# A 512-column matmul over the high and low part of the first 256 tokens, with the key products of the decode moved to eighths 55 to 62

## What is computed

```python
h = RMSNorm_pre(x)
p = h @ w_in                     # one projection, 2048 x 8208
q_a, k_a, v_a, z_a, qkv_b, z_b, beta_in, a_in = split(p)
# mixer A: dilated windows (128,1), (512,4), (2048,16), 8 heads x 128, rotary on 32 dims;
#          the samples attend to cached keys and values
# mixer B: gated DeltaNet, 8 heads: causal conv of width 4 + SiLU on q/k/v, delta rule in chunks
o_a, o_b = mixer_A(...) * silu(z_a), mixer_B(...) * silu(z_b)
y = x + RMSNorm_post(concat(o_a, o_b) @ w_out)
```

## Time and profile before

| | |
|---|---|
| runs | 1330.28, 1328.22, 1330.18 us; median 1330.18 |
| the profiled execution's own time | 1330.15 us |
| its span, first to last instruction | 1328.3 us |
| TensorE matmuls | 1258.6 us busy, 95%, 10094 instructions |
| VectorE | 768.2 us, 58% |
| ScalarE | 543.2 us, 41% |
| GpSimd | 288.5 us, 22% |
| DMA | 151.71 MB, 82695 packets, mean 114 GB/s |

### The profile page before, as it was taken

One profiled execution on the slowest core, in us unless ns is written; L12 is line 12 of the kernel. 1 busy time (PEld: TensorE's weight loads), 2 busy tenths in 40 slices (PEclk: granted clock), 3 DMA queues, 4 the chain that ended last, 5 costly groups with the idle time before them and its releaser, 6 DMA issues. The chain is left out here.

```text
span 1328.3 us, 28169 instructions
## 1 busy us (share of the span) xinstructions
PE 1258.6 (95%) x10094; PEld 1212.4 (91%) x10094; DVE 768.2 (58%) x1872; ACT 543.2 (41%) x1472; POOL 288.5 (22%) x271
## 2 busy tenths in 40 slices
PE   4999998999999999999999999999999998899997
PEld 4989998999899989998999899989998997889997
DVE  6466367537653765377537653765376556474445
ACT  6352344434443444344434443444344444412210
POOL 1123112321232123212321232123112311122210
PEclk9999999999999999999999999999999998899998
DMA  6331434243324342434243324332434254312353
GB/s 226 92 96 51 137 105 146 55 146 108 129 55 147 106 130 58 138 113 136 66 138 111 122 66 138 116 118 66 138 117 132 66 185 143 98 65 95 95 192 129
DMA packets 82695, 151.71 MB, mean 114 GB/s; under 512 B 8793, under 2 KB 27330, under 8 KB 81026
## 3 DMA queue, kind: packets, MB, share of 16 engines
q1 hardware_dynamic: 72222, 144.87, 34.2%
q10 hardware_dynamic: 10384, 5.50, 1.6%
HBM read 132.20 MB, written 17.27 MB: 113 GB/s over the span
## 5 line engine op out<-in xcount | busy, mean ns | idle before, releaser
L553 PE MATMUL PJ<-h_hi,w_hi 128*128 128x264 f32 (+1 forms) x2432 | 723.3, 297 | 1.2 <-ACT memx L981 1.2
L554 PE MATMUL PJ<-h_lo,w_hi 128*128 128x264 f32 (+1 forms) x2432 | 689.9, 284 | 0.0
L555 PE MATMUL PJ<-h_hi,w_lo 128*128 128x264 f32 (+1 forms) x2432 | 688.3, 283 | 0.0
L553 PEld LDWEIGHTS PJ<-h_hi,w_hi 128*128 128x128 f32 x2432 | 462.5, 190 | 17.8 <-issue 12.4
L554 PEld LDWEIGHTS PJ<-h_lo,w_hi 128*128 128x128 f32 x2432 | 462.7, 190 | 2.8 <-issue 1.7
L555 PEld LDWEIGHTS PJ<-h_hi,w_lo 128*128 128x128 f32 x2432 | 460.9, 190 | 0.0
L1858 POOL TENSOR_TENSOR w_lo<-w_raw,w_hi 128x512 fp32r<-128x512 f32 x160 | 210.1, 1314 | 887.8 <-ACT w_hi L954 887.8
L954 ACT ACTIVATE w_hi<-w_raw 128x512 fp32r<-128x512 f32 x320 | 197.7, 624 | 102.7 <-PE PJ L555 84.1
L1364 DVE TENSOR_TENSOR w_lo<-w_raw,w_hi 128x512 fp32r<-128x512 f32 x160 | 114.0, 718 | 117.5 <-ACT w_hi L954 113.9
L981 ACT ACTIVATE memx<-PJ 128x264 f32<-128x264 f32 (+2 forms) x130 | 49.2, 379 | 71.9 <-PE PJ L555 60.5
L1223 ACT ACTIVATE mem<-MX 128x256 f32<-128x256 f32 x48 | 18.4, 384 | 116.6 <-PE MX L755 116.0
(11 more groups left out here) (317 smaller groups left out, 1618.8 us busy)
## 6 DMA issues: line engine op xcount, KB each, us to landing
w_raw<-in_w_in SPq DMA_DIRECT2D x256, 256.0 KB, 2.7
w_raw<-in_w_out SPq DMA_DIRECT2D x64, 256.0 KB, 2.8
kv<-in_cache_win_k SPq DMA_DIRECT2D x24, 512.0 KB, 3.6
kv<-in_cache_win_v SPq DMA_DIRECT2D x16, 512.0 KB, 3.8
mem<-in_x_prompt SPq DMA_DIRECT2D x4, 1024.0 KB, 10.4
S<-in_state_delta SPq DMA_DIRECT2D x8, 512.0 KB, 3.5
out<-S SPq DMA_DIRECT2D x8, 512.0 KB, 3.7
out<-mem ACTq DMA_DIRECT2D x16, 256.0 KB, 3.3
```

Source lines behind the costliest of these rows:

```text
L553: pe.matmul(out, wh, h_hi[:, k, tok], start=k == 0, stop=False)
L554: pe.matmul(out, wh, h_lo[:, k, tok], start=False, stop=False)
L555: last = pe.matmul(out, wl, h_hi[:, k, tok], start=False, stop=k == KT - 1)
```

## The change

1. h_hi and h_lo become one tensor h2, and for each k of a first half one matmul of 512 columns (the 256 tokens' high and low part side by side) takes the place of L553 and L554. It fills the whole bank; w_lo with h_hi adds to its first 256 columns. It holds for all tiles of the projections but the first two and the interleaved ones at the start of the output projection. VectorE adds the two halves of the bank by a reduce at segment 4 (`half_out`) and takes over the guards; ScalarE's copy of the first half goes. TensorE waits for `proj_half` in place of `proj_sb` there.
2. New keys, values and convolution rows are written by channel straight from xk, xv and xq by SyncE; the samples' q by an access pattern that swaps its two dimensions. L650, L651, L652, L658, L702 and the ScalarE copies and DMAs behind them go. The host transposes the outputs.
3. The key products of a head stand at steps 55 to 62 of its own stretch (`decode_keys`), with their loads moved in SyncE's queue. The decode after the last head starts 14 steps earlier (`late=-14`).
4. VectorE's list has mix_b ahead of own_b. Row 9 of the gated matrix gets another buffer and is loaded early; rows 10 to 14 and the value loads are issued ahead of the weight load of the same step.

```diff
-ROW_GROUPS = ((0, 1, 2, 3, 4, 5, 6, 8), (9, 10, 11), (12, 13, 14))
+ROW_GROUPS = ((0, 1, 2, 3, 4, 5, 6, 8, 9), (10, 11), (12, 13, 14))
-        h_hi = sb("h_hi", [P, KT, TT], F32R)
-        h_lo = sb("h_lo", [P, KT, TT], F32R)
+        h2 = sb("h2", [P, 2, KT, TT], F32R)
+        h_hi, h_lo = h2[:, 0], h2[:, 1]
...
+                both = PJ[:, 0, :].rearrange("p (a t) -> p a t", a=2)
+                wide = half == 0 and not (isinstance(T, int) and T < 2)
...
+                    elif not end:
+                        pe.matmul(both, wh, h2[:, :, k, tok], start=k == 0, stop=False)
+                        last = pe.matmul(ps, wl, h_hi[:, k, tok], start=False, stop=False)
...
+            def half_out(h, j):
+
+                T = NT * h + (T_H + j)
+                dst, off = DST[j]
+                guard(h, j)
+                dve.wait_ge(s["proj_ps"], made(T, 0))
+                dve.tensor_reduce(dst[:, off:off + SPLIT], PJ[:, 0, :].rearrange("p (a t) -> p t a", a=2), AX.X,
+                                  ALU.add).then_inc(s["proj_half"], 1)
...
+                        if seg == 4 and not (isinstance(h, int) and h == 0 and j == 0):
+                            half_out(h, j)
...
+            def attn_rows(h):
+                yield from idle(47)
+                if not first:
+                    sp.wait_ge(s["pv_sum"], h)
+                keys(0)
+                yield from idle(2)
                 sp.wait_ge(s["qrow_out"], 16 * h + 16)
+                sp.dma_start(qb[:], scratch_q[h].rearrange("b d -> (b d)").partition_broadcast(P)).then_inc(s["qb_in"], 16)
...
+            def conv_out(h):
+
+                yield from idle(9)
+                for j in range(3):
+                    sp.wait_ge(s["proj_sb"], 16 * h + (2 * j + 4))
+                    sp.dma_start(c_new[h, j], xq[:, TP:3 + TT]).then_inc(s["crow_out"], 16)
+                    yield from idle(8)
+
+            def attn_out(h):
+
+                yield from idle(46)
+                sp.wait_ge(s["q_ok"], h + 1)
+                sp.dma_start(scratch_q[h].rearrange("b d -> d b"), xa[:, TP:TT],
+                             allow_slow_non_contiguous=True).then_inc(s["qrow_out"], 16)
+                yield from idle(7)
+                sp.wait_ge(s["k_ok"], h + 1)
+                sp.dma_start(k_new[h], xk).then_inc(s["k_out"], 16)
+                yield from idle(5)
+                sp.wait_ge(s["proj_sb"], 16 * h + 16)
+                sp.dma_start(v_new[h], xv).then_inc(s["v_out"], 16)
...
-                stretch(h, [tail_a(h - 1), attn_decode(h - 1, sums=(24, 4, 3)), own_b(h), own_a(h), mix_b(h), mix_q(h),
-                            delta_decode(h)])
+                stretch(h, [tail_a(h - 1), mix_b(h), own_b(h), own_a(h), mix_q(h), delta_decode(h),
+                            attn_decode(h - 1, sums=(22, 4, 3)), decode_keys(h)])
...
-            work = [later(tail_a(NH - 1)), attn_decode(NH - 1)]
+            work = [later(tail_a(NH - 1)), attn_decode(NH - 1, late=-14)]
```

More of the change, by code:

```diff
@@ L498, in _ @@
             for n in range(40):
+                step(work)
                 if n % 2 == 0 and n < 8 * PARTS:
@@ L502, in _ @@
                     load_out(slot + 2, p)
-                step(work)
             over(work)
@@ L542, in _, with segment @@
         def _(pe):
-            def segment(T, par, half, q, first=False):
+            def segment(T, par, half, q, first=False, out=False):
                 if half == 0:
@@ L559, in segment, with project @@
                     last.then_inc(s["w_used"], 1)
-            def project(T, par, work, first=False):
+            def project(T, par, work, out=False):
                 for half in range(2):
                     for q in range(NQ):
-                        segment(T, par, half, q, first)
+                        segment(T, par, half, q, out=out)
                         step(work)
@@ L690, in tail_a @@
                 last.then_inc(s["attn_ps"], 1)
-            def own_b(h):
-                for j in range(3):
-                    yield from idle((11, 7, 8)[j])
-                    pe.wait_ge(s["proj_sb"], 16 * h + (2 * j + 4))
-                    if j == 0 and (not isinstance(h, int) or h > 0):
-                        pe.wait_ge(s["vtok_ok"], 2 * h)
-                        pe.wait_ge(s["crow_ok"], 3 * h)
-                    elif j > 0:
-                        pe.wait_ge(s["crow_ok"], 3 * h + j)
-                    pe.transpose(MD[0:11, 1, 0:P], xq[:, 3 + TP - 3:3 + TT], ident[:]).then_inc(s["crow_ps"], 1)
             def mix_b(h):
@@ L845, in delta_decode, with attn_decode @@
                               stop=True).then_inc(s["d_outer"], 1)
-            def attn_decode(hh, sums=12):
-                yield from idle(17)
-                pe.wait_ge(s["vtok_ok"], 2 * hh + 2)
+            def attn_decode(hh, late=0, sums=12):
+                yield from idle(17 + late)
+                pe.wait_ge(s["vtok_ok"], hh + 1)
                 pe.wait_ge(s["qkp"], hh + 1)
@@ L976, in copy_out @@
             def copy_out(T, half, dst, off=0):
+                late = not (isinstance(T, int) and T < 2)
                 act.wait_ge(s["proj_ps"], made(T, half))
+                if late:
+                    act.wait_ge(s["proj_half"], T - 1)
                 o = off + half * SPLIT
@@ L1171, in own_b @@
             def own_b(h):
-                for j, m in enumerate((1, 2, 0)):
-                    yield from idle((11, 4, 5)[j])
-                    act.wait_ge(s["crow_ps"], 3 * h + j + 1)
-                    if j > 0 or not isinstance(h, int) or h > 0:
-                        act.wait_ge(s["crow_out"], 32 * (3 * h + j))
-                    act.activation(rows, MD[0:11, 1, 0:P], ACT.Copy).then_inc(s["crow_ok"], 1)
-                    yield
+                for j in range(3):
+                    yield from idle((12, 5, 6)[j])
                     act.wait_ge(s["conv_ok"], 3 * h + j + 1)
@@ L1723, in attn_decode @@
                     last.then_inc(s["red"], 1)
-                yield
-                yield
+                    yield
+            def attn_decode(hh, late=0, sums=(9, 1, 4)):
+                yield from idle(17 + late)
                 dve.wait_ge(s["sc_T"], hh + 1)
@@ L1799, in y_half @@
                     link(dve.tensor_tensor(sz[:, tok], PJ[:, half, 0:WIDTH[half]], y_ch[:, j, tok], ALU.add))
+                elif wide and half == 0:
+                    link(dve.tensor_reduce(sz[:, tok], PJ[:, 0, :].rearrange("p (a t) -> p t a", a=2), AX.X, ALU.add))
                 else:
```

238 lines of the change are left out of this document (105 added, 133 removed).

## The result

The changed kernel takes **1377.12 us** (median of 4 runs, 1376.50 to 1378.01), the kernel before 1330.23 in the same rounds (4 runs): ratio 1.0354, 95% interval 1.0336 to 1.0372. I had forecast 1280, in 1266 to 1301. The profiled run took 1376.50 us, its span is 1374.6.

The account below looks back on a forecast made before the run. The prediction took TensorE, busy for 95% of the span, to bound the kernel. Its terms, -25.4 - 8.8 - 5.8 + 2.8 + 3.6 - 6.5 - 9.9 = -50.0, took 1330.15 us to 1280, range 1266 to 1301.

Parts of the forecast that it names:

- Part 1: Projection tiles: merging two 256-column matmuls into one of 512 saves 21.5 ns, 1184 times, 25.4 us in all.
- My own counter-evidence: Evidence for the rivals on projection matmuls: surplus stays, 1290 us (chance 0.25), or no saving, 1303 us (0.05).
- SyncE's new DMAs: SyncE's queue: the added output DMAs of each head wait for things already due and cost 0.
- The rival of the late query: Samples' q, 1024 single elements, delays VectorE at step 55: slower, 1335 us; chance 0.05 together with late sums.
- Part 5: Wait at L727, once per head: TensorE arrives 0.45 us earlier and waits that much longer, 3.6 us given back.
- Part 3: Key products moved into their own head's steps: L854's wait goes, 5.8 us saved, at no cost to the recurrence.
- Part 4: VectorE's sums of the bank halves delay the block inverse's first step (L755) by 0.35 us a head: +2.8 us.
- Part 2: TensorE, per head: ten transposes taken out, 80 in all at 0.11 us, 8.8 us saved.
- Part 6: Behind the last head: two holes, each followed by half clock, close, saving 6.5 and 9.9 us.
- the first hole: Tail, TensorE stopped at 1101.23 because row 9 of the gated matrix came late; loading it early saves 6.5 us.
- TensorE waits for the recurrence: Sign of being wrong in kind: TensorE waiting for the recurrence in steps 55 to 62; no size given.
- The output tiles: Output projection tiles, nothing but matmuls, should shrink from 11.48 us to near 11.1; otherwise wrong in kind.

Follow-up runs that it names:

- e17: e16 with 14 of 16 merged pairs of each wide half issued as three 256-column matmuls again: 1288.35 us.
- e18: e16 run again unchanged, in the same rounds as e17: 1285.32 us.
- e1: The changed kernel with the samples' query written as 128 rows of 32 bytes instead of 1024 single elements: 1322.26 us.
- e3: The changed kernel, single elements kept, with the first key load moved from step 47 to step 51, behind the query's broadcast: 1339.38 us.
- e16: e11 with VectorE's L1561 (the scaled values) also moved ahead of the third convolution's second half: 1284.77 us.
- e12: e11 with row 9 of the gated matrix loaded late again and the last head's decode 14 steps later again: 1301.08 us.
- e11: e1 with VectorE's second half of the third convolution and ScalarE's sigmoid of that convolution each one step later: 1291.89 us.
- e8: The changed kernel with the query's single-element write issued at step 51, behind k's swap, and the broadcast and second key load behind it: 1394.78 us.
- e13: e11 with an added unread write per head of 128 single elements into 512 contiguous bytes: 1338.58 us.
- e14: e11 with an added unread write per head of 1024 single elements, each 64 bytes from the next: 1293.68 us.
- e15: e11 with the query written a second time per head, unread, in 128 rows of 32 bytes: 1292.08 us.
- e9: The changed kernel writing only the first sample's query, 128 single elements in one 512-byte row, and reading that row back eight times: 1394.96 us.

## Why the prediction was wrong, step by step

**Part 1, the merged matmul: mis-sized, 3 to 6 us in place of 25.4.** TensorE in the output tiles, 15 pairs of 512 + 256 columns from the first row to the last:

```profile
1240.38 0.40 PE L589 MATMUL PJ<-h,w_hi 128*128 128x512 f32 x1
1240.61 0.28 PE L590 MATMUL PJ<-h,w_lo 128*128 128x256 f32 x1
...
1245.63 0.28 PE L592 MATMUL PJ<-h,w_lo 128*128 128x256 f32 x1
```

5.25 us / 15 = 350.0 ns a pair, 5.2 ns less than three matmuls, where I had 21.5; x 1184 are 6.2 us, and 3.0 were measured in e17 and e18 for 1036 pairs. 512 columns take 350.0 - 118.4 = 231.6 ns, 18.3 above the bare stream (the starts themselves lie 234 and 117 ns apart, median of 1110 pairs). The step that failed is the inference from the earlier trace rows: slow passes of ordinary 32-bit data and a stretch at half clock have no surplus, so I held that a long stream hides it. The surplus grows with the columns instead, from 11.7 to 18.3 ns. My own counter-evidence, that 264 columns cost 2.3 ns more than 256, was right and deserved more than 0.30. By the rule that I cited from the Trainium skill (TensorE: Matmul & The Clock Gate, Back-to-back issue gap) the merge would save 3 us. That it comes near is no support for it: its level is off at both sizes (109.2 ns against 118.4, 215.8 against 231.6), and the section gives it for a matmul by itself and says that at few columns it counts too little, since it leaves out the weight loads.

**SyncE's new DMAs, "0": the step that cost the forecast.** The term was 0; with rows of 32 bytes in its place (e1) the kernel is 54.9 us faster. I looked at when they are issued and who waits for them, and priced the one for q at 33 ns a piece. The rival of the late query had the cause and the sign, but the wrong place (step 55 instead of the swap at step 49), and a price by the piece, for which I gave it 0.05. The row behind the 33 ns is a mean over a queue whose pieces have 530 bytes on average (5.50 MB / 10384); it says nothing about elements that lie side by side. The elements' own packets take 9 ns each by the trace, less than I had; what they cost shows behind them. The DMA of e3, from 278.5 to 287.5 us, which is behind the elements' write (issued at 276.64), in 40 slices:

```profile
DMA  3000000000320410000000000122820240003302
```

and of the changed kernel from 281.5 to 290:

```profile
DMA  3162602206000502017034900940508006902099
GB/s 21 19 96 77 58 19 39 39 0 58 19 19 0 39 19 39 19 19 58 39 39 19 96 19 0 58 19 19 39 19 39 0 0 58 39 19 19 19 77 58
```

Each digit is the busy share of the 16 engines in tenths. In e3 most slices are empty while a weight load (8.4 us to landing), the swap and the query's write are all under way. In the changed kernel the engines count as 41% busy in this stretch, but the keys trickle at a mean of 34 GB/s: its 70 packets over 512 bytes take 0.79 us each on average. In e1 the like stretch, from 274 to 277.5 us, moves 168 GB/s, with 0.18 us for such a packet. So a busy share does not show this stall, whether it is low or high; the time to landing does.

**Part 5, L727's wait: right in kind, 7.7 us in place of 3.6, and the clock left out.** I held that VectorE's chain keeps its 9.0 us, since the work is the same set in another order. It takes 9.8, from L1514 at 359.50 to L745 at 369.32. VectorE there:

```profile
365.96 0.23 DVE L1521 TENSOR_SCALAR memx<-cw 128x8 f32<-128x8 f32 x1
366.23 1.44 DVE L1524 SCALAR_TENSOR_TENSOR memx<-cw,memx 128x8 f32<-128x8 f32 x2
367.71 0.23 DVE L1524 SCALAR_TENSOR_TENSOR memx<-memx,cw 128x8 f32<-128x8 f32 x1
```

and GpSimd:

```profile
366.39 1.26 POOL L1855 TENSOR_TENSOR w_lo<-w_raw,w_hi 128x512 fp32r<-128x512 f32 x1 [6.80 <-ACT w_hi L972]
```

The second of the two small operations takes 1.18 us instead of 0.23 and ends when GpSimd's operation ends (367.65). The Trainium skill (GPSIMD Engine Reference, Specifications) says that GpSimd shares its SBUF interfaces with VectorE, and that instructions with two SBUF inputs contend; the trace agrees, 1.18 us against 0.23 for an operation with two such inputs. It is so in 7 of the 8 heads. The kernel before has the same meeting in 7 heads (1.27 us, from 337.30 in the head of the earlier trace rows), but in the second convolution, before its chain starts at 343.04; the new order moved it into the chain. The longer wait also costs more clock. Before:

```profile
350.00:355.00 5.00, 3.00 (x17) 3.01 (x18) 3.06 (x7) 3.75 (x10) 1.28 (x1) 0.79 0.08 33
355.00:360.00 5.00, 5.00 (x38) 5.00 (x38) 1.38 (x2) 1.65 (x4) 1.27 (x1) 0.87 0.43 138
```

and e1, where nothing else is in the way (the number behind the engines is the granted clock):

```profile
352.00:357.00 5.00, 2.93 (x14) 2.93 (x15) 3.71 (x9) 2.25 (x4) 0.39 (x1) 0.59 0.16 56
357.00:362.00 5.00, 5.00 (x33) 5.00 (x33) 1.39 (x2) 1.19 (x3) 1.27 (x1) 0.72 0.37 105
```

In 10 us of each, (0.21 + 0.13) x 5 x 2 = 3.4 us at half clock before and (0.41 + 0.28) x 5 x 2 = 6.9 in e1: 1.7 us more are lost in this head, about 14 in eight if the others are like it. The whole trace bears this out: over the seven heads between the landmarks the granted clock is 0.991 before and 0.974 in e1, 8.5 and 23.9 us lost, 15 more. I had priced half clock at the tail only.

**Part 3, the key products: right.** L854's wait of 5.8 us went, as said, and the cover that I cost at 0 held: in e1 no wait of the recurrence itself is left.

**Part 4, the sums: right.** 2.8 forecast, 2.3 measured (L773).

**Part 2, the transposes: 4.5 us given back that I had not counted.** 80 of them are gone from the trace; their 8.8 us were not tested alone. But L820 waits 5.7 us in all, where L802 waited 1.2. Before, the end of the recurrence on TensorE:

```profile
290.42 0.39 PE L795 MATMUL MX<-small,mem 128*128 128x128 f32 x2
...
292.29 0.60 PE L657 MATMUL MD<-ident,memx 128*128 128x128 f32 x4
292.72 0.27 PE L658 MATMUL MD<-ident,memx 128*8 128x128 f32 x1
293.15 0.66 PE L802 MATMUL MX<-ident,mem 128*128 128x128 f32 x4 [0.15 <-DVE mem L1628]
```

and now:

```profile
307.92 0.39 PE L813 MATMUL MX<-small,mem 128*128 128x128 f32 x2
...
310.65 0.66 PE L820 MATMUL MX<-ident,mem 128*128 128x128 f32 x4 [0.71 <-DVE mem L1623]
312.59 0.60 PE L687 MATMUL MD<-ident,memx 128*128 128x128 f32 x4
```

Both take 2.73 us from the recurrence's last result to L802 or L820, so VectorE is no slower; it even idles 0.81 us ahead of L1611, so the key products do not delay it. What changed is TensorE's work in between: L658 is gone, and the four transposes of the values, which stay for attention, stand one step later (L687). So these five transposes at 0.11 us ran where TensorE would otherwise have waited: taking them from there saves nothing, and the four that moved cost their time anew. The wait stays in e16 (6.0), so it is not the elements' doing.

**Part 6, the tail: the sum came near, its cause only in part.** 16.4 forecast; 15.6 between the landmarks of the two traces, and this holds part 1 in the output tiles too. e12 undoes both edits and gives back 9.2, not 16.4. From the last landmark to the end pass 240.3 us before, 236.2 in e12 and 226.9 in e11: some 9 us are these two edits, some 4 others. The wait of the last decode is back in e12 (6.2 us), which bears out the decode's part. The wait of the first hole is 1.95 us in e12 as in e11, 2.95 before. So row 9's group is not what shortened it, and my 6.5 for it is not borne out; which other edit did it was not tried.

**The sum again**, for the kernel without the bad write (e1, 42 us above my 1280): part 1 some 19 to 22, the wait at L745 4, the clock behind it some 14, L820 4.5. These make 42 to 45. The tail, about 4 short of my figure beside what part 1 lost there, would make it 46 to 49, so the pieces are estimates and some 4 to 7 us of them are counted twice or made good elsewhere. The bad write adds 55.

Of my signs, "TensorE waits for the recurrence" came true, but at step 53, just ahead of the steps that I named (in e8 at the key products). The output tiles shrank from 11.48 us to 11.42 (L592 to L592, 1245.63 to 1257.05), not to 11.1. Both stood in the text as what would make me wrong in kind.

## What to carry to other kernels

When a change alters the form of a transfer, look at where its pieces fall in the memory and how small they are, and at every transfer issued in the 10 us behind it on any queue, not only at who waits for its data. A price per packet from another shape is no bound for it. Before you take work out of an engine, look whether it covers a wait. Where TensorE has one wait a head, look at what stands ahead of its input in the other engines' queues before you remove matmuls: three small moves in that order gave e1 37 us (1322 to 1285), over ten times what the merge gave. Follow the wait, since it moves to the next engine each time.

## What the runs showed of the hardware that I had not expected

- 128 four-byte pieces, written side by side from 128 partitions, take 9.1 us to land (median, e13) and hold up other queues' transfers (the swaps of k take 7.5 to 9.6 us against 2.0); 1024 such pieces 64 bytes apart, with 512 bytes for each partition, take 4.1 (e14); 128 rows of 32 bytes 1.8 to 2.2 (e15, e1).
- A broadcast of 512 KB that reads one 512-byte row again and again, in pieces of 512 bytes, takes 17.3 us (e9), one that reads 4 KB 3.9 to 6.6. Whether the row or the size of the pieces does it was not tried.
- A matmul of 512 columns of the fast 32-bit type, with its weight load, takes some 232 ns in the output tiles, two of 256 take 236.8.
- A 128x8 operation of VectorE with two inputs from SBUF took 1.18 us beside GpSimd's of 1.26, and 0.23 alone.
